# The first expert's rows: formed in place on the tensor engine instead of fetched by a gather

## The reference

```
h = rmsnorm(x, g_ffn)                      # x: the residual rows, 520 tokens x 1024
g_sel  = argmax of 4 group logits          # one group per token
top 2 of the 8 experts in that group, with weights top_w
for each of 32 experts: act = silu(h @ wg) * (h @ wu);  out += (act @ wd) * c[:, None]
y = x + out
```

## Time and profile before

| | us |
|---|---|
| median of 3 runs | 1216.6 (1216.37 to 1219.7) |
| the profiled execution, whole time | 1217.09 |
| its span, first to last instruction | 1215.2 |
| PE busy / DVE / ACT / POOL | 1050.3 / 441.3 / 246.4 / 299.1 |
| mean granted clock of PE, share of full speed | 0.963 |

### The profile page before, as it was taken

One profiled execution on the slowest core, in us unless ns is written; L12 is line 12 of the kernel. 1 busy time (PEld: TensorE's weight loads), 2 busy tenths in 40 slices (PEclk: granted clock), 3 DMA queues, 4 the chain that ended last, 5 costly groups with the idle time before them and its releaser, 6 DMA issues. The chain is left out here.

```text
span 1215.2 us, 16147 instructions
## 1 busy us (share of the span) xinstructions
PE 1050.3 (86%) x6013; PEld 539.1 (44%) x6013; DVE 441.3 (36%) x1213; ACT 246.4 (20%) x537; POOL 299.1 (25%) x262
## 2 busy tenths in 40 slices
PE   4999899988998999998999869999778777778775
PEld 2554444444444444422356535555444344434442
DVE  4343878787464555422234411111111111011220
ACT  2012111211344454421024301111111101111001
POOL 1023322342354444200200013323222122222211
PEclk9999899989999999998999969999999999999998
DMA  5150222025574533679656679999999999999992
GB/s 184 23 168 27 70 87 96 27 70 182 166 222 144 189 106 104 240 252 377 210 235 253 244 278 395 393 392 397 399 405 399 402 405 399 398 402 399 409 394 69
DMA packets 79858, 304.15 MB, mean 250 GB/s; under 512 B 22706, under 2 KB 22706, under 8 KB 67618
## 3 DMA queue, kind: packets, MB, share of 16 engines
q1 hardware_dynamic: 64354, 273.47, 59.0%
q0 software_dynamic: 9824, 16.98, 4.9%
q10 hardware_dynamic: 5600, 12.65, 2.8%
HBM read 290.03 MB, written 29.66 MB: 263 GB/s over the span
## 5 line engine op out<-in xcount | busy, mean ns | idle before, releaser
L394 PE MATMUL p_z<-k_w,k_xT 128*128 128x512 f32 (+2 forms) x528 | 214.8, 562 | 4.3 <-DVE p_t L581 3.7
L394 PEld LDWEIGHTS p_z<-k_w,k_xT 128*128 128x128 f32 (+1 forms) x528 | 94.4, 193 | 110.5 <-issue 110.2
L826 PE MATMUL a_G<-k_w,k_xT 128*128 128x512 f32 x256 | 129.5, 630 | 2.5 <-ACT k_x L888 2.5
L2008 DVE TENSOR_TENSOR e_hid<-e_hid,e_G 128x256 f32<-128x256 f32 x32 | 13.5, 421 | 269.3 <-ACT e_hid L1921 269.3
L1926 ACT ACTIVATE e_y<-e_Y,x_share 64x512 f32<-64x512 f32 x64 | 43.7, 683 | 313.0 <-PE e_Y L1811 304.1
L927 POOL TENSOR_TENSOR k_x<-k_x 128x512 f32<-128x512 f32 x64 | 80.5, 1269 | 102.2 <-DVE k_side L990 82.1
L2049 POOL DMA_INDIRECT out_y_p<-e_y,x_table x32 | 45.0, 1407 | 199.3 <-ACT e_y L1926 148.1
L152 POOL DMA_INDIRECT k_rows<-token_rows,x_table x32 | 31.3, 978 | 181.3 <-PE e_TX L1791 171.2
L826 PEld LDWEIGHTS a_G<-k_w,k_xT 128*128 128x128 f32 x256 | 45.1, 197 | 50.3 <-issue 46.2
L1198 PE MATMUL g_ring<-k_w,k_oT 128*128 128x512 f32 x128 | 59.9, 614 | 0.0
L2013 DVE TENSOR_TENSOR e_hid<-e_hid,e_U 128x256 f32<-128x256 f32 x32 | 13.5, 421 | 127.0 <-PE e_U L1797 127.0
(11 more groups left out here) (357 smaller groups left out, 1521.9 us busy)
## 6 DMA issues: line engine op xcount, KB each, us to landing
k_w<-in_w_in SPq DMA_DIRECT2D x11, 2048.0 KB, 8.7
k_xT<-in_w_down SPq DMA_DIRECT2D x11, 2048.0 KB, 43.2
x_page<-in_w_down SPq DMA_DIRECT2D x10, 2048.0 KB, 44.2
x_w_out<-in_w_down SPq DMA_DIRECT2D x10, 2048.0 KB, 44.9
k_w<-in_w_gate SPq DMA_DIRECT2D x8, 2048.0 KB, 42.3
k_w<-in_w_up SPq DMA_DIRECT2D x8, 2048.0 KB, 43.7
k_oT<-in_w_gate SPq DMA_DIRECT2D x8, 2048.0 KB, 42.6
k_side<-in_w_up SPq DMA_DIRECT2D x8, 2048.0 KB, 44.6
```

The lines of the kernel that those rows point to most:

```text
L394: last = nc.tensor.matmul(z[u % 3][0:p, 0:WIDTH[k]], s.xT[:, j, 128 * i:128 * i + p], s.w[:, c % 2, j, 0:WIDTH[k]], start=j == 0, stop=j = ...
L826: last = nc.tensor.matmul(G[u % 2][:], s.xT[:, j, 128 * i:128 * i + 128], s.w[:, q % 2, j, :], start=j == 0, stop=j == KD - 1)
```

## The change

Expert 0's turned rows are formed by PE from `s.x` itself, in five tiles of tokens: for each tile 8 matmuls (`first_rows`) with the rows `s.x` as the stationary operand, read with the step of 8 elements, and as the moving operand a 128x64 matrix `sel` that holds, for each token of expert 0, its rmsnorm scale in the column of its place. `sel` is made on DVE by three operations a tile (`pick_first`). The sum over the tiles stands in a PSUM bank that the two blocks now share (`s.bankT`, one of the banks that turned the merged rows in `merge`, and `TX` in `experts`). Expert 0's gather and turn are gone. SP's load (3, 0), which overwrites `s.x`, waits for the last of these matmuls (`first_made`). At the start of `experts` POOL gathers for experts 1 and 2.

```diff
@@ merge, block.sync
             sp.wait_ge(s.x_stored, 16 * TILES)
             sp.wait_ge(s.h_stored, 16 * TILES)
+            sp.wait_ge(first_made, 1)
             load_expert(sp, io, s, FIRST, 0)
@@ merge, block.tensor
+            def first_rows(i):
+                a, p = order(i), ROWS[i]
+                pe.wait_ge(picked, a + 1)
+                for j in range(KD):
+                    last = nc.tensor.matmul(B[0][:, CAP * j:CAP * j + CAP], s.x[0:p, i, :].rearrange("t (q j) -> t j q", j=KD)[:, j, :],
+                                            sel[0:p, i, :], start=a == 0 and j == 0, stop=a == TILES - 1, skip_group_check=True)
+                if a == TILES - 1:
+                    last.then_inc(first_made, 1)
...
                 last.then_inc(tabled, 1)
+                for tile in between:
+                    first_rows(tile)
                 pe.wait_ge(shares_in, a + 1)
...
             logit(3)
+            first_rows(0)
             rank(3)
-            tables(3)
+            first_rows(1)
+            tables(3, [NT, 2, 3])
@@ merge, block.vector
+            def pick_first(i):
+                a, p = order(i), ROWS[i]
+                dve.wait_ge(rms, a + 1)
+                link(v.tensor_scalar(pick[0:p, :], s.oh[0:p, i, :, 0], rs[0:p, i:i + 1], None, ALU.mult))
+                link(v.tensor_scalar(sel[0:p, i, :], Rk[0:p, 0, 0, :], pick[0:p, 0:1], None, ALU.mult))
+                v.scalar_tensor_tensor(sel[0:p, i, :], Rk[0:p, 1, 0, :], pick[0:p, 1:2], sel[0:p, i, :], ALU.mult, ALU.add).then_inc(picked, 1)
...
             decide(3)
             place(3)
+            pick_first(3)
@@ experts, block.tensor
-            rows(0)
             for e in range(NE):
@@ experts, block.vector
             def spread(e):
-                dve.wait_ge(x_turned, e + 1)
+                if e:
+                    dve.wait_ge(x_turned, e)
@@ experts, block.gpsimd
-            for n in range(2):
-                gather_rows(nc, s, n, s.table[:, n:n + 1])
+            for e in (1, 2):
+                gather_rows(nc, s, e % 2, s.table[:, e:e + 1])
```

More of the change, by code:

```diff
@@ L1082, in merge @@
         ring = [ps(f"ring{n}", [128, W]) for n in range(RING)]
-        B = [ps(f"B{n}", [128, W]) for n in range(2)]
+        B = [s.bankT, ps("B", [128, W])]
+        sel = sb("sel", [128, TILES, CAP])
+        pick = sb("pick", [128, 2])
         prod, aZ, sT = s.prod, s.aZ, s.sT
@@ L1116, in merge @@
          nk_read, sc_ready, max_ready, p_ready, weights, p_turned, a_ready, v_used, o_ready, ov_ready, ext_ready,
-         oq_ready, o_sum, orr_ready, o_rs, oT_ready, ms_ready, zeros_ready) = map(sem, (
+         oq_ready, o_sum, orr_ready, o_rs, oT_ready, ms_ready, zeros_ready, picked, first_made) = map(sem, (
              "made g_exp gs_exp y_read chain merged_ready turned mt_out summed x_done x_in sel_up sel_read nk_ready nk_up "
              "nk_read sc_ready max_ready p_ready weights p_turned a_ready v_used o_ready ov_ready ext_ready "
-             "oq_ready o_sum orr_ready o_rs oT_ready ms_ready zeros_ready").split())
+             "oq_ready o_sum orr_ready o_rs oT_ready ms_ready zeros_ready picked first_made").split())
         (wr_in, wr_ready, x_sq, pool_chain, rms, hn_ready, h_turned, hT_out, logits, differ, decided, weighed, ranked, tab_in, shares_in, tabled,
@@ L1295, in rank, with tables @@
                 last.then_inc(ranked, 1)
-            def tables(i):
+            def first_rows(i):
[6 more added lines that the diff above has]
+                    last.then_inc(first_made, 1)
+            def tables(i, between=()):
                 a, p = order(i), ROWS[i]
@@ L1718, in _ @@
             share(0)
+            pick_first(0)
             add_x(NT, 0)
@@ L1724, in _ @@
             share(1)
+            pick_first(1)
             decide(NT)
@@ L1728, in _ @@
             share(NT)
+            pick_first(NT)
             decide(2)
@@ L1732, in _ @@
             share(2)
+            pick_first(2)
             add_x(3, 1)
@@ L1760, in experts @@
         y = [sb(f"y{n}", [CAP, D]) for n in range(2)]
-        TX, AT = ps("TX", [128, KD, CAP]), s.bankO[:, 0:256].rearrange("p (f t) -> p f t", f=2)
+        TX, AT = s.bankT[:].rearrange("p (j c) -> p j c", c=CAP), s.bankO[:, 0:256].rearrange("p (f t) -> p f t", f=2)
         CT, TB = s.bankO[:, 320:320 + NE], s.bankO[:, 352:352 + 2 * NX]
@@ L1859, in rows @@
             def rows(e):
-                pe.wait_ge(xg_in[e % 2], 16 * (e // 2 + 1))
-                if e:
-                    pe.wait_ge(xT_out, e)
+                pe.wait_ge(xg_in[e % 2], 16 * ((e + 1) // 2))
+                pe.wait_ge(xT_out, e)
                 turn_rows(e % 2).then_inc(x_turned, 1)
             nc.tensor.matmul(CT, s.c[:, C_ONE:C_CM], s.Cpre[:], start=True, stop=True, skip_group_check=True).then_inc(counted, 1)
-            rows(0)
             for e in range(NE):
@@ L1896, in step @@
             def step(pe, b):
-                pe.wait_ge(xg_in[0], b * 16 + NE * 8 + 16)
+                pe.wait_ge(xg_in[0], b * 16 + NE * 8)
                 pe.wait_ge(y_out, b + NE)
@@ L1946, in spread @@
             def spread(e):
-                dve.wait_ge(x_turned, e + 1)
+                if e:
+                    dve.wait_ge(x_turned, e)
                 if e >= 2:
                     dve.wait_ge(u_done, e - 1)
-                v.tensor_tensor(xT[:, e % 2], TX[:], bcast(s.gffn[:], CAP, 2), ALU.mult).then_inc(xT_out, 1)
+                v.tensor_tensor(xT[:, e % 2], TX, bcast(s.gffn[:], CAP, 2), ALU.mult).then_inc(xT_out, 1)
             link = Chain(dve, extra_chain)
@@ L2028, in step @@
             def step(dve, b):
-                dve.wait_ge(x_turned, b + NE + 1)
-                v.tensor_tensor(xT[:, 0], TX[:], bcast(s.gffn[:], CAP, 2), ALU.mult).then_inc(xT_out, 1)
+                dve.wait_ge(x_turned, b + NE)
+                v.tensor_tensor(xT[:, 0], TX, bcast(s.gffn[:], CAP, 2), ALU.mult).then_inc(xT_out, 1)
                 dve.wait_ge(gated, b + NE + 1)
@@ L2056, in _ @@
             for e in range(NE + 1):
-                if e + 2 < NE:
-                    pool.wait_ge(x_turned, e + 1)
+                if e and e + 2 < NE:
+                    pool.wait_ge(x_turned, e)
                     gather_rows(nc, s, e % 2, s.table[:, e + 2:e + 3])
@@ L2070, in step @@
                 pool.wait_ge(y_added, b * 32 + NE * 32)
-                pool.wait_ge(x_turned, b + NE)
+                pool.wait_ge(x_turned, b + NE - 1)
                 nc.gpsimd.tensor_copy(idx[:, 0:1], s.table[:, bass.ds(b + NE, 1)]).then_inc(idx_ready, 1)
@@ L2157, in step_kernel @@
         s.bankO = top.enter_context(nc.psum_tensor("x_O", [128, W], F32))
+        s.bankT = top.enter_context(nc.psum_tensor("x_T", [128, W], F32))
         s.xg = [s.rowbuf[0:CAP, 2 * n + 2:2 * n + 4, :].rearrange("p a w -> p (a w)") for n in range(2)]
```

## The result

| | kernel before | changed kernel |
|---|---|---|
| median, us | 1216.41 (1213.49 to 1219.7, 9 runs) | 1222.72 (1220.25 to 1225.78, 9 runs) |
| profiled execution, us | 1217.09 | 1221.2 |
| its span / mean granted clock | 1215.2 / 0.963 | 1219.4 / 0.969 |

The ratio is 1.0055, with a 95% interval of 1.0042 to 1.0068: 6.7 us slower (5.1 to 8.3). The forecast was 1223.0, which is 6.4 us slower.

A forecast was written before the change was run, and what follows sets the result against it. The prediction took DMA weight transfers as the bound: T at 714.6 less 708.2 gave +6.4 us, 1223.5 against the profiled 1217.1, forecast as 1223.0 because that execution lay 0.5 over the median; range 1213.5 to 1227.5.

The forecast's parts named there:

- The bound: From 725 to 1190 us the DMA engines are always busy, so the end depends on their 7.2 us idle before.
- the rule of the sum: End moves by DMA idle after (T - 700.3), less 7.2 us idle before and 0.65 for one gather: T - 708.2.
- T: Instant the last first_rows matmul ends and SP issues (3, 0): 714.6 us, counted from tile 3's logit loads ending at 694.3.
- What s is: Time s between stationary loads of first_rows: 0.24 us taken for step 8, bounds 0.11 and 0.267, at full clock.
- rival 1: Step costs first_rows loads nothing, 0.11 to 0.13 us apart: 1214 us, 22 in 100; 4 of these for fallen clock, 1221.
- The cover: DVE's pick_first, some 0.75 us a tile, falls in DVE's waits; tile 3's in its 1.16 us token-table wait.
- Behind T: After T, G of expert 0 starts about 1.8 us later, at 716.4; load (4, 0) makes 728 with 5 us spare.
- Rival 2: Half the step penalty on first_rows loads, 0.13 to 0.20 us apart: 1215 to 1219.5 us, 15 in 100.
- Rival 3: Slow first_rows load not hidden beside the previous matmul, 0.24 + 0.055 us: change +11, 1228 us, 8 in 100.
- Rival 4: Chain up to 855 us is PE's, so the end moves with G's start, +2.3 us, 1219; 3 in 100.

The follow-up runs named there:

- tile-0: Changed kernel with first_rows for tile 0 only, expert 0's rows from the other four tiles left out: 1212.45 us, ratio 0.9965 to the kernel before.
- doubled kernel: Changed kernel with the first_rows matmuls of tiles 4, 2 and 3 made twice: 1234.21 us, ratio 1.0153 to the kernel before.
- step-1 kernels: Changed kernel with first_rows' stationary operand read with step 1, expert 0's channels in another order: 1223.13 us; with its weights and gain reordered to match: 1220.94 us.
- right channels: Changed kernel with step 1 in first_rows and expert 0's gate and up weights and gain loaded in natural channel order, output correct: 1220.94 us, ratio 1.0038.
- steps 2 and 4: Changed kernel with first_rows' stationary operand read with step 2 or step 4 in place of 8, one execution each: 1218.75 and 1223.98 us.
- moved loads: Changed kernel with one piece of load (3, 1) right behind the last early load, its other two later, (3, 0) last: 1221.04 us, ratio 1.0032.
- wider operand: Changed kernel with step 1, natural-order expert 0 weights, loads reordered and a 128-column moving operand, half of it zeros: 1211.97 us, ratio 0.9960 to the kernel before.

## Why the prediction was right

**The bound and the rule of the sum** were right: 15.3 us idle where T - 700.3 = 14.3 was forecast, and the 1.0 between them is the 1.0 by which T was short (below); both of before's gaps became one; the tile-0 and the doubled kernel follow the rule from -4.3 to +18.6 us.

**T** came out 21.3 us behind L, forecast 20.3 (714.6 - 694.3). The absolute instant, 712.67, is earlier only because this execution had L 3 us earlier. Term by term:

| | forecast | measured |
|---|---|---|
| tile 0's 16 loads | 3.84 | 695.09 - 691.29 = 3.80 |
| four loads of the rank | 0.44 | 695.92 - 695.09 = 0.83 |
| tile 1's 16 loads | 3.84 | 699.74 - 695.92 = 3.82 |
| four loads of the token table | 0.44 | 700.75 - 699.74 = 1.01 |
| the late 48 | 11.5 | 712.38 - 700.75 = 11.63 |
| last drain | 0.2 | 712.67 - 712.38 = 0.29 |

**What s is** gave the right number, 0.24, with half of its cause. In the first loads the clock was up (1.00 from 691 to 693), and their distance is the step's. From 694 on it was down, and there step 1 would have given 0.217 as well. The prediction set "clock full" beside step 8 and kept the fallen clock for rival 1 alone ("I expect it to stay up", 4 in 100). That step failed: the clock fell although PE had no pause. One of the prediction's own signs shows it: the token table's four loads, which should have begun 0.11 apart, took 0.95 us. Since both causes make about 0.22 to 0.24, and do not add up (0.242 with both), the number survived. That was luck: nothing in the prediction said that they would not add up. That 1223.0 lies 0.3 from the measured 1222.7 says no more; T was 1.0 us short, and the measured change is known only to 1.6 us.

One of the two rows that led to 0.24 did not say what was read in it. The 207 against 141 ns of the earlier trace rows was taken as the price of step 2, but other loads of 128 columns with step 1 have the longer mean as well, such as those of the merged rows:

```profile
L1228 PEld LDWEIGHTS g_P<-x_w_out,g_mT 128*128 128x128 f32 x64 | 11.8, 190 | 13.5 <-issue 13.4
```

In `first_rows` step 2 cost almost nothing (0.118). The other row, ACT's, has the step of 8 and the factor of two, and that is what PE's loads showed.

The 1.0 us by which T was short is the second and fourth row of the table, the loads of the rank and of the token table at half clock. The fallen clock also means that half clock with step 1, which the prediction priced at s = 0.22 and T = 713 (1221), is what the step-1 kernels ran into: 1220.94 with the right channels.

**The cover** held: `pick_first` ran from 697.15 to 697.98, and DVE then waited 2.88 us for the token table, as PE was in tile 1's matmuls.

**Behind T** G of expert 0 came 2.1 us after it (forecast 1.8), and (4, 0) at 720.09, with room to spare as argued.

**The rivals.** Rival 1 (the step costs nothing) falls at 0.237 against 0.112. Rival 2's half penalty falls by the steps 2 and 4: it is none or all. Rival 3 (load not hidden beside the pass) would be 0.29; 0.237 to 0.242 stood. Rival 4 falls as told.

On the clock, the Trainium skill ("TensorE: Matmul & The Clock Gate", "Why this matters for your kernels") advises against idle gaps between bursts of matmuls, so that the clock does not drop. In the changed kernel the pause ahead of the rank was filled and the clock dropped all the same, with PE busy 1.00 of each microsecond from 690 on. The last pause before the drop was this one of 0.48 us, 4.8 us ahead of it:

```profile
689.11 0.63 PE L1274 MATMUL g_ring<-k_c,k_x 128*128 128x128 f32 x4 [0.48 <-DVE k_x L1542]
```

## What to carry to other kernels

Where an operation is taken off a path, ask what the replacement holds: here the rows' memory, which the next weight load needed, and each microsecond of holding it was a microsecond of the end, while the gather it replaced was worth some 4. Where two causes give the same number, taking away one shows little: step 1 alone won 2 us (with the right channels) and the moved loads alone 3, and with the wider operand as well they made the change 11 us faster. A matmul chain of many stationary loads and narrow passes can lose the clock while it is never idle, so bound its loads at both clocks.

## What the runs showed of the hardware

- A float32 stationary load of 128 columns starts every 0.112 us with step 1, 0.118 with step 2, 0.233 with step 4 and 0.237 with step 8; at half clock 0.217 with step 1 and 0.242 with step 8.
- The granted clock fell from 1.00 to 0.50 between 693 and 695 us in the changed kernel with PE busy all the time, some 2.5 us into the step-8 loads; with step 1 at 699 to 700, 5 us into them and behind a pause of 0.72 us, and in the kernel with the right channels 3.3 us into them. It stayed down until G of expert 0. With 128 columns a pass it was down for 3 us and came back without any pause of the matmuls.
- With an indirect gather issued 0.1 us after PE's last matmul of the block, the barrier held PE for 8.93 us instead of 0.60, until some 0.6 us after the gather had landed.
